# Experts in chunks of 64 slots on halves of TensorE's columns, in plain fp32

## The reference

```python
sizes = jnp.bincount(flat_e, length=N_EXPERTS).astype(jnp.int32)
xs = t[tok].astype(w_gate.dtype)
hid = jax.nn.silu(lax.ragged_dot(xs, w_gate, sizes)) * lax.ragged_dot(xs, w_up, sizes)
y = lax.ragged_dot(hid, w_down, sizes)
y = y * gate.reshape(-1)[order][:, None].astype(y.dtype)
```

## Time and profile before

| | |
|---|---|
| median of 3 executions | 2076.99 us |
| the profiled execution's own time | 2079.55 us |
| its span, first to last instruction | 2077.8 us |
| granted TensorE clock, mean of the span | 0.929 of 2.4 GHz |
| busy: TensorE matmul | 1763.5 us (85%) |
| busy: TensorE weight load | 1455.0 us (70%) |
| busy: VectorE | 1296.8 us (62%) |
| busy: ScalarE | 961.8 us (46%) |
| moved by DMA | 376.64 MB, mean 181 GB/s |

### The profile page before, as it was taken

One profiled execution on the slowest core, in us unless ns is written; L12 is line 12 of the kernel. 1 busy time (PEld: TensorE's weight loads), 2 busy tenths in 40 slices (PEclk: granted clock), 3 DMA queues, 4 the chain that ended last, 5 costly groups with the idle time before them and its releaser, 6 DMA issues. The chain is left out here.

```text
span 2077.8 us, 40338 instructions
## 1 busy us (share of the span) xinstructions
PE 1763.5 (85%) x15365; PEld 1455.0 (70%) x15366; DVE 1296.8 (62%) x1885; ACT 961.8 (46%) x1490; POOL 209.0 (10%) x267
## 2 busy tenths in 40 slices
PE   3998879899696799999919988899986939999992
PEld 0898678788454588888818986788873527888882
DVE  2388255556445696896663883556662368999674
ACT  2244523233312786786432454333332138888651
POOL 0000022222000100000020001212220010000001
PEclk7999999999797899999959999999997969999996
DMA  7221093420313798897643111331004059999854
GB/s 313 71 82 44 31 358 126 154 102 2 107 59 152 285 384 340 335 401 286 228 153 98 55 44 51 127 125 52 3 2 145 31 209 385 397 398 397 355 199 165
DMA packets 112110, 376.64 MB, mean 181 GB/s; under 512 B 14730, under 2 KB 35490, under 8 KB 86374
## 3 DMA queue, kind: packets, MB, share of 16 engines
q1 hardware_dynamic: 83310, 303.85, 39.2%
q10 hardware_dynamic: 20168, 39.89, 5.0%
q0 software_dynamic: 8496, 30.94, 4.0%
HBM read 332.87 MB, written 41.78 MB: 180 GB/s over the span
## 5 line engine op out<-in xcount | busy, mean ns | idle before, releaser
L1955 DVE TENSOR_TENSOR expert_w_lo<-shared,expert_w_hi 128x2048 fp32r<-128x2048 f32 x192 | 430.6, 2285 | 44.6 <-ACT expert_w_hi L1897 44.3
L1897 ACT ACTIVATE expert_w_hi<-shared 128x2048 fp32r<-128x2048 f32 x192 | 360.6, 1915 | 42.4 <-PEq L141 37.8
L1839 PE MATMUL ps<-expert_w_hi,expert_x_hi 128*128 128x512 f32 x592 | 232.3, 392 | 5.1 <-DVE expert_x_lo L1951 5.1
L1840 PE MATMUL ps<-expert_w_lo,expert_x_hi 128*128 128x512 f32 x592 | 232.0, 392 | 0.0
L1841 PE MATMUL ps<-expert_w_hi,expert_x_lo 128*128 128x512 f32 x592 | 232.0, 392 | 0.0
L1839 PEld LDWEIGHTS ps<-expert_w_hi,expert_x_hi 128*128 128x128 f32 x592 | 112.2, 190 | 29.3 <-issue 5.9
L1841 PEld LDWEIGHTS ps<-expert_w_hi,expert_x_lo 128*128 128x128 f32 x592 | 112.1, 189 | 23.5
L1840 PEld LDWEIGHTS ps<-expert_w_lo,expert_x_hi 128*128 128x128 f32 x592 | 112.1, 189 | 23.2
L1875 PE MATMUL ps<-expert_w_hi,expert_hid_hi 128*128 128x512 f32 x296 | 118.5, 400 | 2.2 <-ACT expert_hid_hi L1929 1.2
L1011 POOL TENSOR_TENSOR mixer_NTb<-mixer_Bt,consts_sb 128x256 f32<-128x256 f32 x120 | 88.4, 760 | 286.3 <-DVE mixer_Bt L1286 222.7
L1876 PE MATMUL ps<-expert_w_lo,expert_hid_hi 128*128 128x512 f32 x296 | 115.4, 390 | 0.0
(11 more groups left out here) (344 smaller groups left out, 3741.1 us busy)
## 6 DMA issues: line engine op xcount, KB each, us to landing
shared<-in_w_gate SPq DMA_DIRECT2D x64, 1024.0 KB, 7.1
...
y_table<-expert_y ACTq DMA_DIRECT2D x37, 512.0 KB, 8.8
...
```

Source lines behind the costliest of these rows:

```text
L1839: pe.matmul(bank, hi, w_hi[:, j, w], start=first, stop=False)
L1840: pe.matmul(bank, hi, w_lo[:, j, w], start=False, stop=False)
L1897: act.activation(w_hi[:, j, :], raw[:, j, :], ACT.Copy).then_inc(w_hi_done, 1)
L1955: dve.tensor_tensor(w_lo[:, j, :], raw[:, j, :], w_hi[:, j, :].bitcast(F32), ALU.subtract).then_inc(w_lo_done, 1)
```

## The change

A chunk has CH = 64 slots instead of 128. The 64 turned tokens are the stationary operand in one half of the array's columns, and the two halves of the array take two different halves of the weight's columns, so that an output of 64 x 512 lies in PSUM as 128 x 256. The splits into hi and lo go: all products are plain fp32 matmuls. An expert's last chunk, when it holds at most CN = 32 tokens, runs "narrow": four strips of 32 columns, for the four quarters (gate and up, two halves each) at once, and the down product in four quarters of its width. The tail phase computes a flag for each expert, R.wide, which each engine's sequencer loads and branches on. Weights lie in two buffers, one for even and one for odd experts, and are used where they land. The loop over experts takes two experts a pass, and the loop over chunks has NF - 1 = 9 passes. Several waits get a semaphore count behind them (sem_inc(passed, 1)). The y rows of a chunk go out in four stores. The diff, cut to its core:

```diff
-MAXC = 2 * T // P + NE - 1
+CH, CN = 64, 32
+NF = T // CH
+MAXC = 2 * T // CH + NE - 1
...
+    parts["places"] = np.broadcast_to(i[:, 0:CH], (P, CH))
+    parts["bounds"] = np.broadcast_to(np.arange(MAXC + 1)[None, :] * CH, (P, MAXC + 1))
+    parts["floors"] = np.broadcast_to(np.array([-1] + [c * CH for c in range(1, NF)])[None, :], (P, NF))
...
                 if l == 0:
-                    dst = A.y_table.rearrange("(p c) n -> p (c n)", p=P).rearrange("p (m n) -> p m n", n=ZERO)
-                    act.dma_start(dst, G.zero[:, :].unsqueeze(1).to_broadcast([P, MAXC * D // ZERO, ZERO])).then_inc(G.y_zero, 16)
+                    dst = A.y_table.rearrange("c n -> (c n)").rearrange("(p m n) -> p m n", p=P, n=ZERO)
...
+                ch.link(dve.tensor_tensor(tmp2[:, 0, :], base[:, 1:], base[:, 0:NE], ALU.subtract))
+                ch.link(dve.tensor_tensor(tmp2[:, 4, :], G.ps[:, BX, NT * NE:(NT + 1) * NE], tmp2[:, 0, :], ALU.subtract))
+                dve.tensor_scalar(R.wide[:, :], tmp2[:, 4, :], float(CN - CH), None, ALU.is_gt)
...
+        odd = ph.sb("odd_weights", [P, PIECES, PIECE])
+        w = (R.raw, odd)
+        FH, OH, OQ, HQ = FF // 2, D // 2, D // 4, KF // 2
+        xg = ph.sb("xg", [CH, D])
+        xT, hT = ph.sb("xT", [P, KD * CH]), ph.sb("hidT", [P, KF * CH])
+        sg, hid = ph.sb("sg", [P, FH]), ph.sb("hid", [P, FH])
+        y = ph.sb("y", [P, OH])
+        cur = ph.sb("cur_idx", [CH, 1], I32)
...
-            def expert(e, final):
-                n = eng.value_load(R.chunks[0:1, bass.ds(e, 1)], min_val=1, max_val=NT)
+            def expert(i, s):
+                e = i * 2 + s
+                wide = eng.value_load(R.wide[0:1, bass.ds(e, 1)], min_val=0, max_val=1)
+                n = eng.value_load(R.chunks[0:1, bass.ds(e, 1)], min_val=1, max_val=NF)
                 base = eng.value_load(R.base[0:1, bass.ds(e, 1)], min_val=0, max_val=MAXC - 1)
                 with eng.If(n > 1):
-                    with eng.Fori(0, NT - 1) as c:
+                    with eng.Fori(0, NF - 1) as c:
                         with eng.If(n > c + 1):
-                            chunk(e, nc.s_assert_within(base + c, 0, MAXC - 1), False, final)
-                chunk(e, eng.value_load(R.last[0:1, bass.ds(e, 1)], min_val=0, max_val=MAXC - 1), True, final)
-
-            with eng.Fori(0, NE - 1) as e:
-                expert(e, False)
-            expert(NE - 1, True)
+                            chunk(i, s, nc.s_assert_within(base + c, 0, MAXC - 1), False, True)
+                k = eng.value_load(R.last[0:1, bass.ds(e, 1)], min_val=0, max_val=MAXC - 1)
+                with eng.If(wide > 0):
+                    chunk(i, s, k, True, True)
+                with eng.If(wide < 1):
+                    chunk(i, s, k, True, False)
+
+            with eng.Fori(0, NE // 2 - 1) as i:
+                expert(i, 0)
+                expert(i, 1)
+            expert(NE // 2 - 1, 0)
+            expert(NE // 2 - 1, 1)
 
...
-                with sp.Fori(0, NE - 1) as e:
-                    for j in range(PIECES):
-                        sp.wait_ge(w_lo_done, e * PIECES + (j + 1))
-                        sp.dma_start(raw[:, j, :], piece_of(A, l, e + 1, j)).then_inc(raw_in[j], 16)
+                for j in range(PIECES):
+                    sp.sem_inc(w_in[0][j], 16)
+                    sp.dma_start(odd[:, j, :], piece_of(A, l, 1, j)).then_inc(w_in[1][j], 16)
+                with sp.Fori(0, NE // 2 - 1) as i:
+                    for s in range(2):
+                        for j in range(PIECES):
+                            sp.wait_ge(used[s][j], i + 1)
+                            sp.dma_start(w[s][:, j, :], piece_of(A, l, i * 2 + (2 + s), j)).then_inc(w_in[s][j], 16)
...
+                def turn(k):
+                    pe.wait_ge(gathered, k * 16 + 16)
+                    pe.sem_inc(passed, 1)
+                    for n in range(KD):
+                        tr = pe.transpose(turned[:, n * CH:(n + 1) * CH], xg[:, n:D:KD], G.c("ident")[0:CH, 0:CH])
+                    tr.then_inc(xt_p, 1)
+
+                def hid_turn(k, m, wide):
+                    pe.wait_ge(hid_done, k * 2 + (m + 2 if wide else 3))
+                    pe.sem_inc(passed, 1)
                     for n in range(HQ):
-                        q = m * HQ + n
-                        tr = pe.transpose(hid_turned(m)[:, n * P:(n + 1) * P], hid[:, q:FF:KF], G.c("ident"))
+                        for r in range(2):
+                            tr = pe.matmul(hid_turned(m)[half(r), n * CH:(n + 1) * CH], hid[half(r), m * HQ + n:FH:KF],
+                                           G.c("eye")[half(r), :], start=True, stop=True)
                     tr.then_inc(ht_p, 1)
...
+                def gate_up(i, s, last):
                     for n, done in ((0, g_p), (1, u_p)):
                         for q in range(KD):
-                            j = 2 * n + q // 4
+                            j, at = 2 * n + q // 4, q % 4 * FF
                             if q % 4 == 0:
-                                pe.wait_ge(w_lo_done, e * PIECES + (j + 1))
-                            at = slice(q * P, (q + 1) * P)
-                            mm = product(G.ps[:, n, :], x_hi[:, at], x_lo[:, at], j, q % 4 * FF, q == 0, q == KD - 1)
+                                pe.wait_ge(w_in[s][j], i * 16 + 16)
+                            for r in range(2):
+                                mm = pe.matmul(G.ps[half(r), n, 0:FH], xT[:, q * CH:(q + 1) * CH],
+                                               w[s][:, j, at + r * FH:at + (r + 1) * FH], start=(q == 0), stop=(q == KD - 1))
                             if last and q == 3:
-                                mm.then_inc(half_used, 1)
+                                mm.then_inc(used[s][2 * n], 1)
                         mm.then_inc(done, 1)
-                    turn(k + 1, 0, 4)
-                    hid_turn(k, 0)
-                    turn(k + 1, 4, 6)
-                    hid_turn(k, 1)
-                    turn(k + 1, 6, KD)
-                    pe.wait_ge(ya, k + 1)
-                    pe.wait_ge(yd, k + 1)
+
+                def gate_up_narrow(i, s, last):
+                    for q in range(KD):
+                        if q % 4 == 0:
+                            for j in (q // 4, 2 + q // 4):
+                                pe.wait_ge(w_in[s][j], i * 16 + 16)
+                                pe.sem_inc(passed, 1)
+                        for r in range(4):
+                            n, h = r % 2, r // 2
+                            at = q % 4 * FF + h * FH
+                            mm = pe.matmul(G.ps[strip(r), 0, 0:FH], xT[:, q * CH:q * CH + CN], w[s][:, 2 * n + q // 4, at:at + FH],
+                                           start=(q == 0), stop=(q == KD - 1))
+                            if q == 3 and r >= 2:
+                                mm.then_inc(used[s][2 * n], 1)
+                            if q == KD - 1 and r >= 2:
+                                mm.then_inc((g_p, u_p)[n], 1)
+
+                def chunk(i, s, k, last, wide):
+                    pe.wait_ge(xT_done, k + 1)
+                    pe.wait_ge(hid_done, k * 2 + 1)
+                    pe.sem_inc(passed, 1)
+                    (gate_up if wide else gate_up_narrow)(i, s, last)
+                    turn(k + 1)
+                    hid_turn(k, 0, wide)
+                    hid_turn(k, 1, wide)
+                    pe.wait_ge(y_done, k + 1)
                     for q in range(KF):
-                        j, at = 4 + q // 2, slice(q * P, (q + 1) * P)
+                        j, at = 4 + q // 2, q % 2 * D
                         if q % 2 == 0:
-                            pe.wait_ge(w_lo_done, e * PIECES + (j + 1))
+                            pe.wait_ge(w_in[s][j], i * 16 + 16)
                         if q % HQ == 0:
-                            pe.wait_ge(h_hi_done, k * 2 + (q // HQ + 1))
...
+                            pe.wait_ge(hT_done, k * 2 + (q // HQ + 1))
+                            pe.sem_inc(passed, 1)
+                        if wide:
+                            for r in range(2):
+                                mm = pe.matmul(G.ps[half(r), 5, :], hT[:, q * CH:(q + 1) * CH], w[s][:, j, at + r * OH:at + (r + 1) * OH],
+                                               start=(q == 0), stop=(q == KF - 1))
+                        else:
+                            for r in range(4):
+                                mm = pe.matmul(G.ps[strip(r), 5, 0:OQ], hT[:, q * CH:q * CH + CN], w[s][:, j, at + r * OQ:at + (r + 1) * OQ],
+                                               start=(q == 0), stop=(q == KF - 1))
                         if last and q == 1:
-                            mm.then_inc(half_used, 1)
+                            mm.then_inc(used[s][4], 1)
+                    mm.then_inc(y_p, 1)
...
+                def chunk(i, s, k, last, wide):
                     act.activation(warm[:, :], G.eps[:, :], ACT.Silu)
```

(60 more changed lines are left out.)

152 lines of the change are left out of this document (36 added, 116 removed).

## The result

The changed kernel takes 2279.5 us (median of 4, 2275.48 to 2288.25), the kernel before 2076.16 us (2073.97 to 2077.26): a ratio of 1.099, 95% interval 1.095 to 1.102. It is slower by 203 us. Of the forecast (2285 us, 2145 to 2445) size and direction held; what is inside the sum has to be looked at term by term.

What follows compares the result with a forecast made beforehand. TensorE was taken to bound the expert loops. Loops of 847 us against 688 (+159), the clock +50 and small items -4, on 2079.55 us, gave 2285 us, range 2145 to 2445.

Steps and rivals of the forecast that it cites:

- The bound and what hides it: Expert loops, kernel before: TensorE busy nearly throughout, its sequencer's work between chunks just hidden by 5.5 us of down product.
- Chunk counts and streaming: Expert loops: 42 wide and 15 narrow chunks stream 511 us in all, against 605 us for 37 chunks before.
- rival 2: Matmuls on array halves and strips run one after the other: 57 chunks of 23.4 us, 2725 us in all; chance 0.03.
- Idle passes: Loop over an expert's chunks: 155 empty passes at 0.74 us; 8.5 us from down product to next chunk with two chunks.
- Middle gap: Inside a chunk, between gate/up and down product: 2.3 us for a wide chunk, 3.0 us for a narrow one.
- Between experts: At an expert's end: next chunk begins 5.5 us (wide) or 5.8 us (narrow) behind the down product's start, for sequencer work.
- The clock: Expert loops: lower granted clock behind the new gaps costs 50 us, bounds 0 and 110.
- The narrow chunks: An expert's last chunk on four strips: 12.25 us as a single chunk, against 14.7 us for a wide one.
- Rival 1: Between chunks: queued matmuls keep the array busy until the sequencer's branches are through, 2053 us in all; chance 0.12.
- Rival 3: Expert loop body of 1500 TensorE instructions is loaded anew each pass: 144 us on top, about 2430 us; chance 0.07.

Runs made afterwards that it cites:

- e2: The kernel before with its loop over an expert's chunks at 9 passes instead of 4: 2107.8 us, ratio 1.015.
- e1: The changed kernel with the loop over an expert's chunks at 2 passes instead of 9: 2175.6 us, 1.047 of the kernel before.
- e11: The changed kernel with that loop counted by a register, n - 1 passes and no If inside: 2166.1 us, 1.043 of the kernel before.
- e4: The changed kernel without narrow chunks, no flag loaded, the last chunk always wide: 2238.4 us, 1.079 of the kernel before.
- e12: The changed kernel without narrow chunks, with one packed load per expert and a register-counted loop over chunks: 2122.5 us, 1.023 of the kernel before.

## Why the prediction was right

- **The bound and what hides it.** The sequencer's work between chunks of the kernel before was said to be "hidden by the 5.5 us that the down product streams. Only just": right, shown by e2.
- **Chunk counts and streaming.** Right to 1% for the wide chunks, and to 4% for gate/up of the narrow ones (3.3 us at full clock in e1, for 3.45). That halves and strips stream at once in wide fp32 (against rival 2) is in the trace: 64 records in 7.1 us.
- **Idle passes.** Right: 8.43 us for 8.5, and 104 to 113 us are gained by leaving them out (e1, e11).
- **Middle gap.** 2.4 us for 2.3. The narrow one was 0.6 us short: Silu and products were priced from rows of other shapes at 0.37 and 0.75 us, and a latency between each pair was left out. 15 x 0.6 = 9 us.
- **Between experts.** Too high, and this is the step that failed. "About 0.8 us behind the first down matmul for a wide chunk, 1.1 for a narrow one. Then ... 4.7 us": behind a wide chunk whose first down matmul starts at 968.63, the sequencer leaves at 969.00 and TensorE's next matmul starts at 973.18, so 0.37 and 4.2 us. That the hand-over waits for the second half of the turned hidden values was right, but this half is there 0.3 us behind the first down matmul and not 0.8 (narrow: the sequencer leaves at 0.45 to 0.85 us for 1.1); and where the next expert has several chunks, the load of its last chunk's number stands behind the loop over chunks and not in the way. 17 wide ends are 0.95 us shorter than forecast and 15 narrow ones 1.6: 40 us. Two of the wide ends are 5.6 and 8.7 us longer than the others, for long branches that the sum put at nothing: 14 us of the 40 come back.
- **The clock.** 66 us for 50, within its bounds. This and the gaps above nearly cancel the last point: 847 us of loops without the clock were forecast and 825 measured, 897 with it and 891 measured. That the total fell within 6 us is part luck.
- **The narrow chunks.** The sum treated them as a gain (12.25 us for 14.7). They are a loss of 38 us in the loops (e4): they bring the flag's load and branches to all 32 experts and the bare Silu, every one of the 15 ran partly at the low clock, and some 15 us are long branches that came with their code.
- **Rivals.** Rival 1 needed the array busy until the sequencer is through; at an expert's wide end the array has 3.1 us left to stream and the sequencer 4.2 us to do. Rival 3 was said to have 1500 instructions in the loop and 144 us of stops. The changed kernel has 1312 records of matmuls and loads there, and 15 us of stops, at first passes. The same rival at 2080 records costs 350 us. The Trainium skill (Runtime: NRT & Kernel Launch, Instruction fetch mechanics) gives TensorE's code buffer as 2048 instructions. The runs agree: loops of 832, 1248, 1312 and 1344 records, with the control around them, did not stop in every pass; 2016 and 2080 did, and at some 20 control instructions for each copy of a chunk 2016 records come to over 2048 too. The same section has a taken branch stall when its target lies outside a window of two pages; on TensorE the runs don't bear this out, for the jump back over 1344 records didn't stop.

By the runs, the 203 us in the loops come apart so: e12 against before, +48 us, is the tiling in plain fp32 itself (no run separates the two), with the sequencer hidden (57 x 12.82 against 37 x 18.6); e4 against e12, +118, is idle passes and loads with the clock that they cost; the changed kernel against e4, +38, the narrow chunks and their code. The tiling alone streams 12 us less (57 x 10.4 = 593 against 605) and pays 57 gaps of 2.4 us for 37 of 1.9, +66 us. No version of it beat the kernel before; a shorter middle gap would be needed, and that wasn't tried.
